# Taking out TensorE filler matmuls and reordering the matmul queue of the late mixers

## The reference

```python
x = layer_norm(ALPHA * x + mixer(x), ...)            # twice, layers 1 and 2
x = layer_norm(ALPHA * x + square(relu(x @ w1)) @ w2, ...)
...
a = rms_norm(h, ln_mix_pre)
proj = a @ w_in                                      # split into the inputs of four mixers
y_a = s5_mixer(...)      # state space, gelu, gate, rms norm
y_b = hgrn2_mixer(...)   # chunked linear recurrence with decays, head-wise rms norm
y_c = fox_mixer(...)     # attention with forget gates
y_d = mlstm_mixer(...)   # matrix LSTM: qk scores * weights, values, normaliser
h = h + rms_norm(concat(y_a, y_b, y_c, y_d) @ w_out, ln_mix_post)
a = rms_norm(h, ln_ffn_pre)
h = h + rms_norm((silu(a @ gate) * (a @ up)) @ down, ln_ffn_post)
```

## Time and profile before

| | |
|---|---|
| time, median of 3 runs | 2244.32 us (2244.11 to 2244.55) |
| the profiled execution | 2244.32 us |
| its span, first to last instruction | 2242.5 us |
| PE busy | 2114.2 us, 94% |
| DVE busy | 1237.6 us, 55% |
| ACT busy | 820.1 us, 37% |
| mean granted TensorE clock | 0.978 |

### The profile page before, as it was taken

How to read it: one execution, slowest core, us unless ns; L and a number is a source line. 1 busy time by engine, 2 the same in 40 slices (tenths; PEclk the granted TensorE clock), 3 DMA queues, 4 the chain that set the end, 5 groups by cost and what they waited for, 6 DMA issues and landing times. The chain is left out here.

```text
span 2242.5 us, 30140 instructions
## 1 busy us (share of the span) xinstructions
PE 2114.2 (94%) x12280; PEld 1686.0 (75%) x12280; DVE 1237.6 (55%) x1696; ACT 820.1 (37%) x1294; POOL 262.7 (12%) x268
## 2 busy tenths in 40 slices
PE   7899988999999989999999999999998789999996
PEld 6776876787887768888778788877666567878875
DVE  5547665643343376666573444357768737533544
ACT  3443313542232244444352323335233544322321
POOL 0000001100000100000020790020553010000002
PEclk9999998999999999999999999999999989999998
DMA  6110001232232222222123222323211042223321
GB/s 225 66 65 31 2 3 58 87 101 94 94 103 76 94 66 76 75 68 74 39 93 104 90 94 96 102 85 122 66 57 44 2 139 84 90 84 113 101 71 64
DMA packets 51675, 179.20 MB, mean 80 GB/s; under 512 B 5785, under 2 KB 5785, under 8 KB 51281
## 3 DMA queue, kind: packets, MB, share of 16 engines
q1 hardware_dynamic: 47712, 165.45, 22.7%
q10 hardware_dynamic: 3328, 8.13, 1.0%
q0 software_dynamic: 496, 3.69, 0.4%
HBM read 172.51 MB, written 4.21 MB: 79 GB/s over the span
## 5 line engine op out<-in xcount | busy, mean ns | idle before, releaser
L1114 DVE TENSOR_TENSOR w_lo<-w_raw,w_hi 128x1024 fp32r<-128x1024 f32 (+1 forms) x320 | 411.8, 1288 | 728.7 <-ACT w_hi L1107 728.5
L1212 PE MATMUL banks<-xh,w_hi 128*128 128x512 f32 x1560 | 625.8, 401 | 4.6 <-PEq L213 3.6
L1214 PE MATMUL banks<-xh,w_lo 128*128 128x512 f32 x1560 | 610.6, 391 | 0.0
L1213 PE MATMUL banks<-xl,w_hi 128*128 128x512 f32 x1560 | 610.1, 391 | 0.0
L1107 ACT ACTIVATE w_hi<-w_raw 128x1024 fp32r<-128x1024 f32 (+1 forms) x320 | 328.6, 1029 | 717.5 <-PE banks L1214 686.5
L1212 PEld LDWEIGHTS banks<-xh,w_hi 128*128 128x128 f32 x1560 | 294.8, 189 | 84.1 <-issue 21.2
L1214 PEld LDWEIGHTS banks<-xh,w_lo 128*128 128x128 f32 x1560 | 294.2, 189 | 63.2
L1213 PEld LDWEIGHTS banks<-xl,w_hi 128*128 128x128 f32 x1560 | 294.9, 189 | 58.8 <-issue 1.7
L1212 PE MATMUL banks<-hh,w_hi 128*128 128x512 f32 x688 | 271.8, 395 | 11.7 <-DVE w_lo L1114 4.8
L1213 PE MATMUL banks<-hl,w_hi 128*128 128x512 f32 x688 | 269.4, 392 | 0.0
L1214 PE MATMUL banks<-hh,w_lo 128*128 128x512 f32 x688 | 269.3, 391 | 0.0
(11 more groups left out here) (503 smaller groups left out, 2642.1 us busy)
## 6 DMA issues: line engine op xcount, KB each, us to landing
w_raw<-in_w SPq DMA_DIRECT2D x128, 512.0 KB, 3.3
w_raw<-in_w_gu SPq DMA_DIRECT2D x44, 512.0 KB, 3.3
w_raw<-in_w_c_in SPq DMA_DIRECT2D x40, 512.0 KB, 3.3
w_raw<-in_w_ab_in SPq DMA_DIRECT2D x27, 512.0 KB, 3.4
w_raw<-in_w_in SPq DMA_DIRECT2D x25, 512.0 KB, 3.4
w_raw<-in_w_down SPq DMA_DIRECT2D x16, 384.0 KB, 3.0
w_raw<-in_w_down SPq DMA_DIRECT2D x16, 320.0 KB, 2.8
w_raw<-in_w_ab_out SPq DMA_DIRECT2D x8, 512.0 KB, 3.3
```

Source lines behind the costliest of these rows:

```text
L1114: dve.tensor_tensor(lo[:, 0:n], core.raw[u % RAW][:, 0:n], hi[:, 0:n].bitcast(F32), ALU.subtract).then_inc(core.split_ready, 1)
L1212: pe.matmul(bank, hi[:, w], src.xh[:, kk, :], start=kk == 0, stop=False)
L1213: pe.matmul(bank, hi[:, w], src.xl[:, kk, :], start=False, stop=False)
L1214: mm = pe.matmul(bank, lo[:, w], src.xh[:, kk, :], start=False, stop=last)
```

## The change

Three things. (1) `keep_busy` is deleted, with its calls in `LayerNorm.pe_tail` (and the wait on `s.pre` ahead of it), in `RmsPost.pe_tail` and in the late mixers. (2) In PE's list of the late mixers most `mlstm.score(i)` move forward, so that scores and `heads` alternate; `score(1)` moves back behind `spans(0)` and `scan.total`. (3) In ACT's list `hgrn.decay_begin` moves back from behind `span(4)` to behind `span(5)`.

```diff
-def keep_busy(core, pe, bank, n):
-
-    for _ in range(n):
-        pe.matmul(core.psum[bank], core.const("ident"), core.const("chunk"), start=True, stop=True)
-
 class LayerNorm:
...
         pe.matmul(core.psum[SQUARE_BANK], mean, core.line[SQ1][:], start=False, stop=True).then_inc(s.e2, 1)
-        pe.wait_ge(s.pre, KD - 2)
-        keep_busy(core, pe, SHIFT_BANK, 4)
...
 class RmsPost:
...
         pe.matmul(core.psum[SQUARE_BANK], core.const("mean"), core.line[SQ1][:], start=False, stop=True).then_inc(s.e2, 1)
-        if self.late:
-            keep_busy(core, pe, SHIFT_BANK, 4)
...
 late_mixers, scalar:
             mlstm.weight(act, 2)
             hgrn.span(act, 4)
-            hgrn.decay_begin(act)
             norms.square(act, 4)
             mlstm.floor(act, 0)
             mlstm.floor(act, 1)
             mlstm.weight(act, 3)
             hgrn.span(act, 5)
+            hgrn.decay_begin(act)
             hgrn.keys_out(act, 1)
...
 late_mixers, tensor:
             mlstm.score(pe, 0)
-            mlstm.score(pe, 1)
-            keep_busy(core, pe, 2, 2)
             hgrn.spans(pe, 0)
             scan.total(pe)
+            mlstm.score(pe, 1)
             hgrn.spans(pe, 1)
+            mlstm.score(pe, 2)
             hgrn.turn_keys(pe, 0)
             hgrn.spans(pe, 2)
             pe.wait_ge(scan.s.inv, 1)
             mlstm.heads(pe, 0)
             mlstm.heads(pe, 1)
-            mlstm.score(pe, 2)
             mlstm.score(pe, 3)
             hgrn.spans(pe, 3)
             hgrn.turn_keys(pe, 1)
+            mlstm.score(pe, 4)
             mlstm.heads(pe, 2)
             hgrn.spans(pe, 4)
             mlstm.heads(pe, 3)
-            mlstm.score(pe, 4)
             mlstm.score(pe, 5)
             hgrn.spans(pe, 5)
+            mlstm.score(pe, 6)
             mlstm.heads(pe, 4)
             norms.total(pe, 4)
             hgrn.products(pe)
+            mlstm.score(pe, 7)
             mlstm.heads(pe, 5)
-            mlstm.score(pe, 6)
-            mlstm.score(pe, 7)
+            mlstm.score(pe, 8)
...
             mlstm.heads(pe, 12)
+            mlstm.score(pe, 15)
             mlstm.heads(pe, 13)
-            mlstm.score(pe, 14)
-            mlstm.score(pe, 15)
             mlstm.heads(pe, 14)
```

More of the change, by code:

```diff
@@ L2928, in _ @@
             hgrn.products(pe)
+            mlstm.score(pe, 7)
             mlstm.heads(pe, 5)
-            mlstm.score(pe, 6)
-            mlstm.score(pe, 7)
+            mlstm.score(pe, 8)
             norms.total(pe, 5)
             mlstm.heads(pe, 6)
+            mlstm.score(pe, 9)
             mlstm.heads(pe, 7)
-            mlstm.score(pe, 8)
-            mlstm.score(pe, 9)
+            mlstm.score(pe, 10)
             hgrn.result(pe)
-            mlstm.score(pe, 10)
             mlstm.score(pe, 11)
@@ L2941, in _ @@
             mlstm.heads(pe, 9)
+            mlstm.score(pe, 12)
             norms.total(pe, 2)
             mlstm.heads(pe, 10)
+            mlstm.score(pe, 13)
             mlstm.heads(pe, 11)
-            mlstm.score(pe, 12)
-            mlstm.score(pe, 13)
+            mlstm.score(pe, 14)
             norms.total(pe, 6)
             mlstm.heads(pe, 12)
+            mlstm.score(pe, 15)
             mlstm.heads(pe, 13)
-            mlstm.score(pe, 14)
-            mlstm.score(pe, 15)
             mlstm.heads(pe, 14)
```

## The result

The changed kernel takes 2264.86 us (median of four runs, 2264.09 to 2269.48) against 2244.22 us for the kernel before (2242.41 to 2244.55): +20.6 us, a ratio of 1.0098, 95% interval 1.0081 to 1.0115. The forecast was 2256.0 us, with a range up to 2261. The direction was right, the size was not: +11.7 us were expected. The profiled execution took 2261.85 us (span 2260.1), 17.5 us more than the one before, at a mean granted clock of 0.971 in place of 0.978.

A forecast was written before the change was run, and what follows sets the result against it. PE's work and holes were taken to bound the kernel. Tails 9.4 us plus late mixers 2.3 us (2.0 lateness, -0.5 scores, 0.8 clock) gave 11.7 us on 2244.32, so 2256.0 us; range 2249 to 2261.

The forecast's parts named there:

- What bounds the kernel: Whole kernel: PE, busy 94% of the span, bounds it; time is the sum of PE's work and PE's holes.
- Part 1: Five tails without fillers: 4.1 us holes, half clock behind all five, 9.4 us; bounds 6.9 to 11.4, 0 if none falls.
- the price: Half clock behind one tail: 2.1 us, between 1.6 (3.4 us dense work) and 2.5 us (5.5 us).
- the allowance: Fourth layer norm's tail: about 1.1 us of its loss falls into PE's wait for w_lo at 1533.86.
- The late fillers: Two fillers before spans(0): removal gives nothing; a fall is likely, covered by DVE, or 1.5 us if not enough.
- I take 2.0: Late mixers: decay_begin behind span(5) makes spans(4) 2.4 us late, or 1.6 if heads run at full clock; 2.0 taken.
- The scores, -0.5 us: Late mixers: moving scores saves 0.4 us of DVE's last wait and 0.1 us in the middle.
- rival C: Late mixers: moved scores remove DVE's 2.4 us of waits and the hole before 1748.70, another 1.5; 2240.4 us, chance 0.02.
- Clock: ... 3.4 us at half clock cost at most 1.6 us there: New 3 us hole before spans(4): a fall costing at most 1.6 us, halved to 0.8 as PE is not dense behind.
- part 2: Late mixers, three edits: 2.3 us, from 0 to 4.5.
- Rival B: Falls last longer in tails, or a second one comes in the late mixers: 17.9 us, 2262 us, chance 0.10.
- no hole over 3 us was free: Argument that the clock will fall in the tails: half clock came after or within all ten such PE holes.

The follow-up runs named there:

- x1_tails: Kernel before without the fillers of the five tails, late mixers unchanged: 2253.10 against 2244.13 us, 1.0037.
- x5_late_fillers: Kernel before without the two fillers in front of spans(0) in the late mixers: 2244.65 against 2243.43 us, 1.0006.
- x6_late_early_decay: Kernel before with new PE order and no fillers in the late mixers, decay_begin still behind span(4), tails unchanged: 2244.97 us, 1.0007.
- x4_order: Kernel before with the new PE order of scores and heads alone, fillers kept and decay_begin early: 2245.18 against 2244.13 us, 0.9999.
- x7_late_filled: Changed late mixers with two fillers kept before spans(0) and two put before spans(4), tail fillers kept: 2247.34 against 2244.84 us for kernel before, 1.0011.
- x3_decay: Kernel before with decay_begin moved behind span(5) and nothing else: 2253.11 against 2244.13 us, 1.0036.
- x2_late: Kernel before with the changed late mixers (no fillers there, new order, later decay_begin), tails unchanged: 2253.96 against 2244.13 us, 1.0045.
- x11_decay_more_fillers: Kernel before with decay_begin behind span(5), two fillers behind spans(3), one right before spans(4): 2247.46 against 2244.41 us, 1.0015.
- x9_decay_filled: Kernel before with decay_begin behind span(5) and two fillers behind spans(3): 2251.58 against 2243.43 us, 1.0037.
- x8_two_per_tail: Kernel before with two fillers instead of four in each of the five tails: 2248.36 against 2243.43 us, 1.0024.
- x13_small_short: Kernel before with 58 small matmuls instead of four dense fillers in each of the five tails: 2244.72 against 2244.84 us, 1.0000.
- x14_dense_behind: Kernel before with decay_begin behind span(5) and three dense fillers right behind spans(4): 2254.24 against 2244.84 us, 1.0034.
- x12_small_fillers: Kernel before with 116 small matmuls instead of four dense fillers in each of the five tails: 2257.93 against 2244.41 us, 1.0063.

## Why the prediction was off, step by step

**What bounds the kernel**: right. What was lost is PE's holes, PE's slower clock and, in the late mixers, more of PE's own time for the same scores.

**Part 1, "5 x 2.1 - 1.1 = 9.4 us"**: right in mechanism, and near in sum partly by luck, since two errors offset each other. x1_tails gave 8.3 us by its ratio and 9.0 by the medians, and the clock fell in all five. By the distances in the changed profile it was 8.5: the price was 1.7 us too high in all (with 1.55 for the fourth tail, whose own can't be read), the allowance 0.8 too high. The price of a fall was the lower bound, 1.55 us, in three tails (3.4 us at half clock) and the upper one, 2.57, in the fifth (5.4 us of dense work at half clock, as at 688.5). The fourth tail's allowance of 1.1 us did not last: the wait for `w_lo` at 1533.86 is gone in the changed profile, as worked out, but 40 us later PE waits 2.98 us for DVE where it had waited 1.50, and the fourth tail still costs 1.28 us, so that 0.3 of the 1.1 us were hidden:

```profile
1573.44 0.66 PE L1705 MATMUL banks<-consts,Y 128*128 128x128 f32 x4 [2.98 <-DVE Y L311]
```

**The late fillers, "taking them out gives nothing"**: the fall was foreseen, and it came; it lasted 6.8 us. In the old order DVE's own work covered it, as worked out (x5_late_fillers from `spans(0)` on). In the changed order it cost 1.0 us by the stages of x6_late_early_decay and x4_order, within the 1.5 us given for a cover that is not enough. The times of these runs don't settle it.

**"I take 2.0" for the lateness of `spans(4)`**: the wait is where it was put, L2138 for L2108, and 2.8 to 3.2 us long. For `spans(4)` itself the term was right: in x7_late_filled, which has the changed order and the full clock, it starts 1.7 us later in its stage (38.81 against 37.09 us), and 3.0 in x3_decay, where the old order gives nothing back. But the stage of x7_late_filled is 3.0 us longer and not 1.7, and the rest arises between `spans(5)` and `result`, where the scores stand alone.

**The scores, -0.5 us**: wrong; some 1.3 us were lost instead. DVE's waits for scores went, as foreseen, and so did the low stretch at 1748.70 that rival C named (in x4_order the clock is at 1.00 from 1722.4 to 1787.1); that gave 1.2 us up to `spans(5)`. All of it is lost at `result`, and x4_order's time is 0.9999 (0.9988 to 1.0009). The prediction took half of a pair's 1.13 us as the price of one score (the "0.5" in two of its terms), where a score alone takes as long as the pair: it put the pairs' coming apart at nothing.

**"Clock: ... 3.4 us at half clock cost at most 1.6 us there; half of it, since PE is not dense behind it: 0.8"**: this is the step that failed, and the one that puts the result outside the range: part 2 was to cost 2.3 us, at most 4.5, and x2_late took 9.8. The new hole in front of `spans(4)` was there and the fall too. But the length of the low stretch was taken from dense work: nothing in the rows of before had small matmuls behind a fall, and I put the dense case there as an upper bound. The trace had such a case, which I overlooked: the low level that begins at 352.6 lasts 17 us, the first 7 of them over matmuls of 64 and 256 columns with short idle times between, ahead of a hole of 5.04 us:

```profile
352.60:359.70 7.10, 4.73 (x49) 0.50 0.00 0
```

The new low stretch lasted 13.6 us in x3_decay and 17 us in the changed kernel, over a part in which every hand-over between PE and DVE goes through `spans`, and it cost about 5 to 6 us in place of 0.8 (x3_decay against x11_decay_more_fillers: 1.0036 and 1.0015, 4.7 us apart; 5.7 us by the two distances behind `spans(4)` in x3_decay's own profile). "PE is not dense behind it" was counted as a relief, when it went with a longer low level and with no slack on the path.

Rival B had named this, a longer or a second fall in the late mixers, at 17.9 us and a chance of 0.10; of its two places the tails did not bear it out and the late mixers did. Its argument against, that nothing under dense work had lasted longer than 5.5 us, was true and did not apply. Together: 8.3 for the tails, 3.0 to 3.4 for `decay_begin`'s wait with the new order, about 5 for the long low stretch, and about 1 for the fillers in front of `spans(0)` make some 17.5, just below the lower end of the ratio's interval (18.2 to 25.8 us). The rest can be the low stretch of the changed kernel, 3.3 us longer than those of x3_decay and x2_late (1758.7 and 1756.2 on, 13.6 us each): the way from `products` to `result` is 9.00 us in the changed kernel and 7.66 in x2_late. That was not isolated.

The Trainium skill's page "TensorE: Matmul & The Clock Gate", section Terms, would price a fall at half of the low time, in holes as well. The trace disagrees most in the fifth tail: the clock is low for 6.8 us, of which PE has no matmul in the 1.2 us from 1868.9, and the tail costs 2.57 us where the rule gives 3.4. In the first three, 3.4 us each, the rule gives 1.7 and the trace 1.53 to 1.57. The time of x1_tails, 8.3 us by its ratio (5.2 to 11.4), is nearer to the prediction's 9.4 than to the 11.7 by the rule. Part 1 of that page calls the low clock the default state from which activity releases the engine, and the point at which it changes something that moves between runs of one kernel. The traces agree with the second: the kernels whose edits lie in the late mixers alone run the same program up to there, and behind the same hole of 3.56 us in front of 1242 the clock falls before and stays at 1.00 in x6_late_early_decay:

```profile
1238.50:1242.00 3.50, 0.00 (x0) 1.00 0.05 12
1242.10:1249.00 6.90, 6.90 (x31) 1.00 0.30 112
```

Of the first they show that being busy 16.28 of 16.90 us, or 10.10 of 10.10 in x9_decay_filled, was not enough here; 10 us of the former and 5 of the latter are small matmuls.

**Still open**: what in a stretch decides. The length of the idle time alone does not (1.38 us before a fall in x9_decay_filled; in x8_two_per_tail 2.28 us with a fall in four tails and 2.23 with none in the fifth; 3.56 us with a fall before and none in x6_late_early_decay). The prediction's "no hole over 3 us was free" held in the trace of before and not in all later ones. Nor is it shown that the size of the matmuls does (x13_small_short speaks against it, with 64 columns and not 32). The difference between small and dense work once the clock is low rests on x3_decay, x2_late, x9_decay_filled and the changed kernel on one side, one profile each, and x14_dense_behind, a single profile too, on the other.

## What to carry to other kernels

Matmuls that compute nothing and hide in a wait are worth what the work behind the wait would lose at half clock: four in a 4 us hole saved 1.7 us a time here, so look at the granted clock before and behind a hole before you tidy it up. Price a fall by what PE does behind it: under dense matmuls it was over after 3.3 to 5.4 us, among small ones handed to and fro with DVE it stayed for 10 to 17 us, on a path without slack. Keep matmuls that use different rows of the array side by side: taken apart, these scores cost PE 12.86 us in place of 6.68. And when an instruction is moved in one engine's list, compute when its first reader wants it: 1.04 us of ACT work put behind a waiting one cost 3 us by itself and another 5 through the clock that the new hole brought down.

## What the runs showed of the chip that was not expected

- Low clock under busy work with many small matmuls: 12.51 of 13.60 us busy at 0.50 in x3_decay, 16.28 of 16.90 us in the changed kernel, 10.10 of 10.10 us in x9_decay_filled. With three dense matmuls put in (x14_dense_behind, one profile) 3.4 us.
- Small matmuls do hold the full clock in a tail: 58 of them in 3.60 us, ratio 1.0000 (0.9991 to 1.0009).
- Holes of 2.4 us went either way in the kernel before; holes of 2.28 us brought the clock down in four cases of four and one of 2.23 us did not (x8_two_per_tail). One of 3.56 us did before and did not in x6_late_early_decay and x12_small_fillers.
- Two scores on different halves of the rows start together and take 1.13 us for 512 columns; one alone takes 1.12 us (x4_order).
- Half clock does not double small matmuls: a block of 64 takes 3.62 us against 2.05.
